# Five of 26 modulation chunks taken in among the projection blocks, the key turned one block sooner, and beta multiplied into the decays ahead of the key products

## The reference, cut to what matters

```python
m = silu(cond) @ w_mod[layer] + b_mod[layer]      # 6 vectors of 1024, for layer 0 and layer 1
sh1, sc1, gt1, sh2, sc2, gt2 = split(m, 6)        # the first 2304 columns are needed ahead of the projection
p = modulate(rms_norm(h, gain), sh1, sc1) @ w_in  # 2832 columns: q, k, v of the delta rule; z, beta, g; the attention
kb = kc * bc                                      # bc is beta; chunks of tokens
lower = where(strict, einsum(kb, kc) * decay, 0)  # (K K^T) * beta * decay
sol = triangular_solve(lower + eye, rhs)          # the kernel forms the inverse, then scans over the chunks
```

## Time and profile before

| | |
|---|---|
| median of 3 runs | 1363.67 us (1362.14 to 1367.49) |
| the profiled execution's time | 1363.14 us |
| its span | 1361.1 us |
| PE busy | 1279.1 us, 94% |
| DVE busy | 869.8 us, 64% |
| ACT busy | 509.7 us, 37% |
| POOL busy | 124.5 us, 9% |
| granted TensorE clock, mean | 0.971 |

### The profile page before, as it was taken

One profiled execution on the slowest core, in us unless ns is written; L12 is line 12 of the kernel. 1 busy time (PEld: TensorE's weight loads), 2 busy tenths in 40 slices (PEclk: granted clock), 3 DMA queues, 4 the chain that ended last, 5 costly groups with the idle time before them and its releaser, 6 DMA issues. The chain is left out here.

```text
span 1361.1 us, 18882 instructions
## 1 busy us (share of the span) xinstructions
PE 1279.1 (94%) x7158; PEld 988.9 (73%) x7158; DVE 869.8 (64%) x1498; ACT 509.7 (37%) x850; POOL 124.5 (9%) x165
## 2 busy tenths in 40 slices
PE   3899979988999998999899999899999999899997
PEld 1687646553888887884588888777878885688886
DVE  1448796543876665795677777399962342777776
ACT  2474256323433444014544444312223321544443
POOL 0043022000000002000000000245520000000000
PEclk9899979999999999998899999899999999899999
DMA  9222367884555542421455555125233233455551
GB/s 391 89 112 77 138 269 287 356 353 180 195 189 186 185 155 70 155 94 47 185 186 185 185 185 198 66 78 185 93 139 127 106 109 123 155 185 185 185 189 58
DMA packets 24946, 225.75 MB, mean 166 GB/s; under 512 B 2737, under 2 KB 2865, under 8 KB 4658
## 3 DMA queue, kind: packets, MB, share of 16 engines
q1 hardware_dynamic: 23328, 220.31, 43.9%
q10 hardware_dynamic: 1554, 4.56, 0.9%
HBM read 223.81 MB, written 1.05 MB: 165 GB/s over the span
## 5 line engine op out<-in xcount | busy, mean ns | idle before, releaser
L872 PE MATMUL psum<-aT_r,arena_r 128*128 128x512 f32 x920 | 327.4, 398 | 1.4 <-DVE arena_r L2191 1.4
L2191 DVE TENSOR_TENSOR arena_r<-ring,arena_r 128x1024 fp32r<-128x1024 f32 x193 | 226.0, 1221 | 112.4 <-ACT arena_r L1599 112.4
L789 PE MATMUL psum<-aT,ring 128*128 128x256 f32 (+1 forms) x1136 | 266.3, 392 | 1.5 <-DVE aT L2148 1.5
L873 PE MATMUL psum<-aT_r,arena_r 128*128 128x256 f32 x920 | 258.2, 281 | 0.0
L789 PEld LDWEIGHTS psum<-aT,ring 128*128 128x128 f32 x1136 | 214.8, 191 | 47.9 <-issue 20.6
L1599 ACT ACTIVATE arena_r<-ring 128x1024 fp32r<-128x1024 f32 x193 | 191.5, 1050 | 149.6 <-PE psum L913 132.4
L913 PE MATMUL psum<-arena_r 128*128 128x512 f32 x876 | 213.5, 392 | 0.0
L872 PEld LDWEIGHTS psum<-aT_r,arena_r 128*128 128x128 f32 x920 | 172.8, 188 | 43.7 <-issue 1.9
L913 PEld LDWEIGHTS psum<-arena_r 128*128 128x128 f32 x876 | 159.5, 188 | 34.8
L873 PEld LDWEIGHTS psum<-aT_r,arena_r 128*128 128x128 f32 x920 | 173.7, 189 | 2.6
L1611 ACT ACTIVATE nrm<-nrm 128x256 f32<-128x256 f32 x76 | 31.8, 418 | 170.8 <-DVE nrm L2205 170.8
(11 more groups left out here) (495 smaller groups left out, 1642.3 us busy)
## 6 DMA issues: line engine op xcount, KB each, us to landing
ring<-in_w_ffn SPq DMA_DIRECT2D x44, 1536.0 KB, 6.5
ring<-in_w_mod SPq DMA_DIRECT2D x32, 1536.0 KB, 8.7
ring<-in_w_ff SPq DMA_DIRECT2D x32, 1024.0 KB, 4.9
ring<-in_w_in_g SPq DMA_DIRECT2D x8, 1536.0 KB, 6.4
ring<-in_w_conf_i SPq DMA_DIRECT2D x8, 1024.0 KB, 4.8
ring<-in_w_hyb_f SPq DMA_DIRECT2D x4, 1536.0 KB, 6.6
ring<-in_w_in_a SPq DMA_DIRECT2D x4, 1536.0 KB, 6.4
ring<-in_w_in_b SPq DMA_DIRECT2D x4, 1536.0 KB, 6.3
```

Source lines behind the costliest of these rows:

```text
L789: last = mm(bank(use)[:, out_at:out_at + rhs(k).shape[1]], weights[:, k * P:(k + 1) * P], rhs(k), start=(k == 0), stop=(k == KT - 1))
L872: mm(bank(use).rearrange("p (a t) -> p a t", a=2), hi, x_both[:, :, k, :], start=(k == 0), stop=False)
L873: last = mm(bank(use)[:, T:2 * T], lo, x_hi[:, k, :], start=False, stop=(k == KT - 1))
L2191: tt(lo, slot(c)[:, at], hi.bitcast(F32), ALU.subtract).then_inc(split_ready, 1)
```

## The change

- Five modulation chunks (`AMONG`, list `_m`) move in `ORDERED` to places among the projection's chunks, all in slot 1, and SP's wait for `att_rope` moves ahead of the first of them. PE takes them after block 9, block 10, block 8, blocks 6 and 7, and the token tile. Six M are struck from `GAPS`, which leaves 22: `"qk"` loses two, `"vn0"`, `"ks2"`, `"vn2"`, `"ds2"` and `"vn3"` one each, and `"ds0"` gains one. The last M is then the last chunk, so `mod_columns(2)` comes when the generators are finished, behind the scan's last products. `mod_take(1)` moves from step 1 to step 0.
- Block 9 moves from ahead of `to_feat` to behind it, on PE and ACT.
- DVE multiplies beta into the decays in eight instructions of 512 columns between `conv5((0,))` and `part_low(10)`; the key products are then multiplied in eight instructions of 512 columns in place of the 32. A buffer of the split (`part_hi[0]`) moves in SBUF.

```diff
+_m = MODS[MOD_CTX:MOD_CTX + AMONG]
+ORDERED = MODS[:MOD_CTX] + HYB_CHUNKS[:6] + _m[:1] + HYB_CHUNKS[6:7] + _m[1:2] + HYB_CHUNKS[7:] + _m[2:]
...
-    "qk": "MSMM", "p5": "M", "q5": "M", "p6": "M", "q6": "SM", "vn0": "TMNSM", "ds0": "TMN", "ks1": "SMV", "vn1": "TMN",
-    "ds1": "SMTM", "ks2": "VMNM", "vn2": "SMTM", "os2": "MNS", "ds2": "TMNM", "oi2": "SMVM", "ks3": "TMNM", "vn3": "MTM",
+    "qk": "SM", "p5": "M", "q5": "M", "p6": "M", "q6": "SM", "vn0": "TMNS", "ds0": "TMNM", "ks1": "SMV", "vn1": "TMN",
+    "ds1": "SMTM", "ks2": "VMN", "vn2": "SMT", "os2": "MNS", "ds2": "TMN", "oi2": "SMVM", "ks3": "TMNM", "vn3": "MT",
...
-                if c == MOD_CTX + len(HYB_CHUNKS):
+                if c == CHUNK[_m[0]]:
                     sp.wait_ge(att_rope, 1)
...
             hyb_features(1, (5,))
-            hyb_features(3, (9,))
             for n in range(4):
                 pe.wait_ge(kq_scaled, n + 1)
                 transposes(USE["to_feat"][n], [ktok[:, n, hh * P:(hh + 1) * P] for hh in range(NH)])
-            hyb_features(3, (10,))
+            hyb_features(3, (9,))
+            next(chunk)
...
-            hyb_features(3, (11,))
-            hyb_features(2, (8, 6, 7))
+            for c, blocks in ((3, (10,)), (3, (11,)), (2, (8,)), (2, (6, 7))):
+                hyb_features(c, blocks)
+                if blocks[0] != 11:
+                    next(chunk)
             hyb_tokens(0)
+            next(chunk)
...
-            features_evac((5, 9))
+            features_evac((5,))
             to_features(range(4))
-            features_evac((10,))
+            features_evac((9, 10))
             conv_silu(5, (4,))
             features_evac((11, 8))
...
             conv5((0,))
+            for n in range(8):
+                d, st = n // 4, n % 4
+                wait_read(dve, USE["decay"][n])
+                src = decay[:, 2 * d + st, :] if st < 2 else U_t[n]
+                ch.mark(tt(quad(U_t[n]), quad(src), bc_in(beta[:, st, 4 * d:4 * d + 4], P), ALU.mult))
             part_low(10)
...
             for st, use in enumerate(USE["kk"]):
                 wait_full(dve, use)
-                for d in range(2):
...
-                    for hh in range(NH):
-                        at = slice(hh * P, (hh + 1) * P)
-                        last = stt(U_t[n][:, at], bank(use)[:, at], beta[:, st, 4 * d + hh:4 * d + hh + 1], src[:, at], ALU.mult, ALU.mult)
...
+                tt(U_t[st], bank(use), U_t[st], ALU.mult).then_inc(ut_ready, 1)
+                freed(tt(U_t[4 + st], bank(use), U_t[4 + st], ALU.mult), use)
...
-                if s == 1:
-                    mod_take(1)
...
+                if s == 0:
+                    mod_take(1)
```

More of the change, by code:

```diff
@@ L80 @@
 MODS = [("mod0", _j) for _j in range(NMOD)] + [("mod1", _j) for _j in range(NMOD)]
-ORDERED = MODS[:MOD_CTX] + HYB_CHUNKS + MODS[MOD_CTX:] + [("hyb_o", _j) for _j in range(4)]
+AMONG = 5
+_m = MODS[MOD_CTX:MOD_CTX + AMONG]
+ORDERED = MODS[:MOD_CTX] + HYB_CHUNKS[:6] + _m[:1] + HYB_CHUNKS[6:7] + _m[1:2] + HYB_CHUNKS[7:] + _m[2:]
+_hyb_end = len(ORDERED)
+ORDERED += MODS[MOD_CTX + AMONG:] + [("hyb_o", _j) for _j in range(4)]
 _rest = len(ORDERED)
@@ L84 @@
 CHUNK = {key: _n for _n, key in enumerate(ORDERED)}
-_hyb_end = MOD_CTX + len(HYB_CHUNKS)
-SLOT_OF = [_n % SLOTS if _n < MOD_CTX else 2 + _n % 2 if _n < _hyb_end else 1 + (_n - _hyb_end) % 3 if _n < _rest
-           else (_n - _rest) % SLOTS for _n in range(len(ORDERED))]
+SLOT_OF = [_n % SLOTS if _n < MOD_CTX else 1 if _key in _m else 2 + HYB_CHUNKS.index(_key) % 2 if _n < _hyb_end
+           else (2, 3, 1)[(_n - _hyb_end) % 3] if _n < _rest else (_n - _rest) % SLOTS for _n, _key in enumerate(ORDERED)]
 TURN_OF = [SLOT_OF[:_n].count(_slot) for _n, _slot in enumerate(SLOT_OF)]
@@ L484, in build @@
         a_lo = [view(x, at, 2, 2 * T) for x, at in ((yT_r, 0), (yT_r, D), (rowbc_r, 0), (diag_r, 0))]
-        part_hi = [arena_r[:, 6144:6144 + D], o_r[:, 0:D], arena_r[:, 14432:14432 + D]]
+        part_hi = [arena_r[:, 4096:4096 + D], o_r[:, 0:D], arena_r[:, 14432:14432 + D]]
         cv = view(arena, 0, 12, 2, T)
@@ L1032, in _, with mods @@
             hs = lambda x, n: (lambda hh: x[:, n, hh * P:(hh + 1) * P])
+            def mods():
+                for run in (1, 2):
+                    for m in range(*MOD_RUNS[run]):
+                        mod_products(m)
+                        yield
+                    mod_columns(run)
+                    if run == 1:
+                        yield
+            chunk = mods()
             hyb_tokens(3)
@@ L1075, in _ @@
             transposes(USE["att_qk"][2], [kctx[:, 0, :], kctx[:, 1, :], rot_a[:, 0, 512:640], rot_a[:, 1, 512:640]])
[L1077 to L1084, removed]
             def scores():
@@ L1126, in pause @@
                         next(beside_steps[step], None)
-            beside_steps = {"M": mods(), "S": scores(), "T": turned(), "V": outputs()}
+            beside_steps = {"M": chunk, "S": scores(), "T": turned(), "V": outputs()}
             pause("qk")
@@ L1816, in pause @@
                     next(beside_steps[step], None)
-            beside_steps = {"M": mod_copies(), "S": weights(), "N": normed(), "T": turned(), "V": outputs()}
+            beside_steps = {"M": itertools.islice(mod_copies(), AMONG, None), "S": weights(), "N": normed(), "T": turned(), "V": outputs()}
             def unit_diagonals(d):
@@ L2340, in _ @@
             conv5((5,))
+            ch.sync()
             for st, use in enumerate(USE["kk"]):
                 wait_full(dve, use)
-                for d in range(2):
-                    n = 4 * d + st
-                    wait_read(dve, USE["decay"][n])
-                    src = decay[:, 2 * d + st, :] if st < 2 else U_t[n]
-                    for hh in range(NH):
-                        at = slice(hh * P, (hh + 1) * P)
-                        last = stt(U_t[n][:, at], bank(use)[:, at], beta[:, st, 4 * d + hh:4 * d + hh + 1], src[:, at], ALU.mult, ALU.mult)
[L2350 to L2353, removed]
+                tt(U_t[st], bank(use), U_t[st], ALU.mult).then_inc(ut_ready, 1)
+                freed(tt(U_t[4 + st], bank(use), U_t[4 + st], ALU.mult), use)
             for use in USE["kk"]:
```

## The result

The changed kernel takes 1375.84 us (median of four runs, 1375.57 to 1378.19) against 1363.23 (1362.14 to 1367.49) for the kernel before on the same chip: ratio 1.0092, 95% interval 1.008 to 1.0105. It is slower by 12.6 us. The span goes from 1361.1 to 1373.8 us, the mean granted clock from 0.971 to 0.968. Medians here are of the fast executions; in the group of experiments 5 to 8 four slow ones (1482 us and more) are left out. (Behind the edits, lines are shifted by 3 to 7: L743 is now L746, L772 L775, L789 L792, L820 L823.)

What follows compares the result with a forecast made beforehand. PE was taken to set the time in all stretches the change touches. Idle-time and clock terms summed to +8.8 us on a span of 1361.1, giving 1372.4 us (+0.65%) from a median of 1363.67; the 8-in-10 range was 1363 to 1378.

Steps and rivals of the forecast that it cites:

- the slow stretch: PE from 185 to 200 us: keeps its clock until the kept 4.21 us wait in q5, -2.0, bounds 0 and -5.
- the chunk waits: In the scan: PE's waits for modulation chunks go, with three M fewer behind "qk", -4.8, bound 0.
- DVE, the multiplications, +4.6: Ahead of part_low(10), beside GpSimd: eight multiplications delay the convolutions and PE's transposes by 4.6 us, bounds 1.1 and 5.0.
- The rival by which DVE's idle time covers them: Ahead of part_low(10): 3.88 us idle covers the multiplications, delay 1.1, no clock fall; +3.8 us, 1367.5; chance 0.18.
- Of its signs one: Between 104 and 115 us: DVE's instructions of 128x512 last 1.2 us or more each if the prediction is right.
- The clock behind that wait, +1.5: PE's first transposes and part of block 5 run at half speed, +1.5 us, range 0 to 3.
- The products, nothing: Key products ahead of the inverse: 8.3 us become 5.2, worth nothing since the inverse waits for ACT's copies.
- The third chunk, +5.7: Behind block 8: PE waits 5.7 us for the third moved chunk, loaded behind the last token chunk; 2.5 otherwise.
- The clock behind it, +2.3: Behind the third chunk's wait: that chunk and some of block 6 at the lower clock, +2.3 us, range 0 to 3.
- The inverse, -2.1, the scores, +0.7: Entry of the scan: PE's 2.08 us wait for the inverse goes; scores wait for ACT's three copies, 0 to 1.4.
- The rival by which wait and slow stretch both go: In q5 and the slow stretch: wait gone, clock stays up; +1.6 us, 1365.3; chance 0.12.
- The end of the scan, +1.9 and +1.0: mod_columns(2) behind the last products: 1.9 us more idle on PE, output products at the lower clock +1.0, range 0 to 2.

Runs made afterwards that it cites:

- experiment 5: Changed kernel with multiplications just ahead of key products, third chunk loaded earlier, last columns ahead of last products, ACT's copies earlier, fifth chunk later: 1357.88 us, ratio 0.9951.
- experiment 6: Experiment 5 with the M of p6 moved to vn0 and SP holding modulation chunk 14 and later loads until q5 ends: 1358.30 us, ratio 0.9948.
- experiment 7: Experiment 5 with the M of p6 moved to vn0 and no load held back, the control of experiment 6: 1359.68 us, ratio 0.9971.
- experiment 8: Changed kernel without GpSimd's rotation of the second token tile and its last additions, for timing only, not computing the layer: 1371.0 us, one run.
- experiment 1: Changed kernel with the eight multiplications moved behind conv5((5,)), just ahead of the key products: 1370.23 us, ratio 1.0041.
- experiment 4: Kernel before with only the eight multiplications ahead of part_low(10) and the key products in eight instructions, no chunk moved: 1369.58 us, ratio 1.0043.
- experiment 10: Experiment 5 with beta and decay multiplied into the key products in 32 instructions, as in the kernel before: 1356.73 us, ratio 0.9946.
- Experiment 2: Changed kernel with the third moved modulation chunk loaded ahead of the last token chunk: 1370.06 us, ratio 1.0041.
- Experiment 3: Changed kernel with a last M added at os3, so mod_columns(2) stands ahead of the scan's last products: 1372.05 us, ratio 1.0055.
- experiment 9: Kernel before with eight multiplications behind conv5((5,)), key products in eight, ACT's copies ahead of the evacuation, no chunk moved: 1361.94 us, ratio 0.998.
- experiment 11: Experiment 10 with one modulation chunk moved from ahead of the products p5 to behind them: 1355.88 us, ratio 0.9931.
- experiment 12: Experiment 11 with one more chunk moved from vn0 to between the two halves of q5: 1359.72 us, ratio 0.9953.

## Why the prediction was right, and where its terms were not

The sum was +8.8 us; +12.6 was measured (12.7 on the span), at the upper end of the 1369 to 1376 of the forecast. Most of the missing 3.8 us lies in two terms, the slow stretch (1.9) and the chunk waits (1.7). Term by term:

- **DVE, the multiplications, +4.6:** right. The wait grew by 4.94 us, up to the bound of 5.0, and experiments 1, 4 and 8 show place, size and cause. (The transposes start 4.38 later, since both engines came to that point 0.56 earlier in this execution.) The rival by which DVE's idle time covers them fell. Of its signs one was too wide: behind GpSimd's end, at 112.46, DVE's instructions last 0.64 us and not 1.2. The row at 108.93 agrees with the rule of the Trainium skill ("SBUF — State Buffer", section "Who interferes with whom"): 4.02 us for 1.28 of work.
- **The clock behind that wait, +1.5:** too high. The level was 0.54 until 130 us, when block 5 had just begun; from the transposes' start to block 5's it is 3.14 us in place of 2.33, so 0.8 were lost.
- **The products, nothing:** right. Experiments 5 and 10 are the same with and without them. The inverse waits for ACT's copies (9.63 us at 162.76), which stand behind the evacuation of block 8, as the working had it.
- **The third chunk, +5.7:** 5.83 measured. **The clock behind it, +2.3:** 1.29 for the chunk and 1.22 for blocks 6 and 7, 2.5 in all. Experiment 2 removes both.
- **The inverse, -2.1, the scores, +0.7:** right (no wait; 0.95 us). `p5` was to start at 200.8 and starts at 200.22.
- **Chunk waits, -4.8:** -3.1. 1.7 us are left, most of it one wait of 1.5.
- **The slow stretch, -2.0:** this is the step that failed. "I keep that wait" of 4.21 us was wrong. The clock did stay up (1.00 from 200 to 208 us, with the DMA engines at 1.00 of their time), as argued, but the waits for nothing that the profile shows are 1.43 + 5.08 = 6.5 us, and the clock falls in the longer one. From the start of `p5` to the scan's first stage it is 26.96 us before (184.46 to 211.42) and 26.86 after (200.22 to 227.08): -0.1. Experiment 4 shows the same with no chunk moved: at the upper level the waits are 6.0 us and not 4.2, and take what the clock gives. The estimate of 5 us for the slow stretch priced PE's work alone, as if the wait did not lengthen when the work ahead of it went faster. The rival by which wait and slow stretch both go fell with it; its own test was that no gap over 1 us shows in `q5`.
- **The end of the scan, +1.9 and +1.0:** 1.8 for the idle time and 1.64 for the products at the lower level. Experiment 3 gives both back. One reading was off without harm to the sum: not three but two of DVE's four additions were done when PE ended, at 299.50; the third starts at 299.44, and the last two are the 1.45 us.

With these, 4.94 + 0.3 + 5.83 + 2.5 - 2.1 - 3.1 + 0.95 - 0.1 + 1.8 + 1.64 = 12.7 us (0.3 is the 0.8 of the transposes less the 0.56 by which PE came earlier). That this meets the span's 12.7 is in part luck, since all its terms lie ahead of the end of the output products, where the marks show less. The difference of the marks says where it lies: `p5` is 15.8 us later, of which 3 x 1.43 = 4.3 is work moved ahead; the output products are 9.9 later (300.95 to 310.88), the transposes behind them 11.6 (309.61 to 321.17), and the end 12.7. So the terms are 1.1 too high up to there, and the last 1.1 come in small steps behind the stretch that was changed. The cause of either is open; four runs of this kernel differ by 2.6.

What moving the chunks was worth was hidden by three stalls that it does not need: 5.6 (place of the multiplications), 5.8 (order of the loads) and 3.8 (columns behind the products). Without them the idea gives 4 to 5 us (6.6 of experiment 5 less 2.8 of experiment 9, on two chips; 5.2 between experiments 9 and 10 on one), and with ACT's order the kernel is 0.5 to 0.7% faster than before. The best measured is experiment 11; its interval and that of experiment 10 overlap.

## What to carry to other kernels

Idle time of DVE beside GpSimd was not free time for work of this kind, which reads and writes SBUF: add up the work of both at free durations before putting anything into it. Where a load queue is in order, a transfer moved forward is as late as the last thing put ahead of it, so place it in the queue by when it is wanted, not by when its buffer is free. And look at what the last wait of a stage has behind it: 0.75 us of work moved behind the last products cost 3.4 in the trace (1.8 and 1.6), half of it through the clock. And a wait whose cause is not known is not a constant: work ahead of it that goes faster may only make it longer.

## What the hardware showed

**PE may run out of instructions.** The waits for nothing in `q5` are, most likely, the arrival of code. Two rows bear on it. The first is a window of the changed kernel that holds the work between the two waits, in the columns above:

```profile
204.50:209.00 4.50, 1.52 (x128) 1.40 (x127) 4.05 (x10) 2.38 (x5) 0.00 (x0) 0.93 1.00 396
```

128 matmuls and 127 weight loads are 255 instructions. It is the same pair in experiments 5, 6, 10 and 11, and in 12, where the chunk's 16 matmuls are among them and the second wait therefore starts at another line (L1160). The second are the rows of the DMA queues (packets, MB, share) from 209.5 to 209.6 us in the changed kernel, and from 194.0 to 194.1 in experiment 6:

```profile
q8 instruction: 1, 0.02, 64.1%
```

```profile
q8 instruction: 1, 0.02, 70.9%
```

A packet of the instruction queue moves 2.4 us before PE goes on at 211.98, and 2.7 before 196.81; ahead of the first waits it is the same (2.3 before 205.38 and before 192.96). With the weights' queue quiet the packet comes before PE has run out, at 194.1, and the wait is 2.00 us; with that queue at its full rate it comes 2.6 us into the wait, which is 5.08. In the kernel before, where PE goes through these products at the lower level, a packet moves at 188.6 and no wait shows behind it; the next moves at 195.0, and PE goes on at 197.46. The 255 instructions themselves are 32x32 products that PE does in 1.5 us at the upper level. That PE waits for this packet is inferred from the time and the count; no run took the packet away. The Trainium skill ("Runtime: NRT & Kernel Launch", section "Instruction fetch mechanics") has blocks of 16 KiB, 256 instructions, with a cost that is mostly hidden: the count agrees. If these packets are what PE waits for, the 6.5 us in the changed kernel do not agree with "mostly hidden" where the instructions are this short and weights are in flight.
